# Hybrid mixer stage with its branches' work in another order, and one side step at every place of the dense stage

## The chip, the cores and the metric

The kernel is one program on one core of a Trainium2 chip. A core has a matrix engine (TensorE, PE in the profile), a vector engine (VectorE, DVE), an activation engine (ScalarE, ACT), a general engine (GpSimd, POOL), a queue engine that only issues transfers here (SyncE, SP), and 16 DMA engines that all of them share. The metric is the device time of one execution in microseconds, the median of several runs; less is better. Each engine runs its own instruction list in order, and they wait for each other through semaphores.

## The reference, cut to what matters

A sequence of 256 tokens of width 1024 passes through a hybrid mixer (gated linear attention beside a sparse attention of three branches), a dense feed-forward layer, a state-space mixer, a mixture of eight experts, and then two layers of another kind. The first four steps share a pattern:

```
def adaln(c, w, b):                      # shift, scale, gate from the condition vector c
    mod = jax.nn.silu(c) @ w + b
    return jnp.split(mod[:, None, :], 3, axis=-1)

for each of hybrid, dense, ssm, moe:
    shift, scale, gate = adaln(c, mod_w, mod_b)          # mod_w is 1024 x 3072
    x = x + gate * layer(rmsnorm(x, w) * (1 + scale) + shift)

gla:  log_alpha = log_sigmoid(lowrank @ gk_up + gk_bias) / 16;  b = cumsum(log_alpha) per chunk of 64
      q_dec = q * exp(b);  k_dec = k * exp(-b);  k_to_end = k * exp(b_end - b)
      o = intra-chunk + state part;  o = rmsnorm(o, out_norm) * silu(r)
nsa:  gate0 * compressed branch + gate1 * branch over selected keys + gate2 * window branch
      (compressed keys and values = gelu(blocks @ w1) @ w2)
mix:  concat([gla, nsa]) @ w_out
dense: (silu(g) * u) @ w_down,  g, u = split(h @ w_gu)   # 1024 -> 2 x 2816 -> 1024
```

## The kernel before, in words

All matrix products are done in two parts to keep float32 accuracy: a weight tile is split into a rounded high part by ScalarE (`split_hi`, uh in the profile) and the remainder by VectorE (`split_lo`, ul), and TensorE makes three products for each tile (high by high, high by low, low by high). The weights arrive in three slots of 2 MB, issued by SyncE; the pieces that are split are called units, and three units are in flight, so ScalarE can split unit n only when TensorE has used unit n - 3.

**The side job.** The shift, scale and gate of a layer need a product of one vector with a 1024 x 3072 matrix. It isn't done on TensorE but woven in beside the stage ahead of it. A generator for each of three engines walks through the jobs hyb, dense, ssm, moe (`side_gpsimd`, `side_vector`, `side_tensor`, lines 955 to 1048). A job has three parts (shift, scale, gate) of 8 chunks: GpSimd's queue loads a chunk of 512 KB into one of three buffers once VectorE is done with the chunk three back, VectorE adds it to `macc` with one instruction of 128x1024, and after the eighth chunk TensorE sums `macc` over the partitions (16 products of one column for shift or scale, `("cols", 0)` and `("cols", 1)`; two wide products for the gate, `"rows"`), and VectorE adds the bias. The bias of the gate is loaded into the buffer that held the last chunk, so only after VectorE has used that chunk.

**Its clock.** The generators go on by one `yield` at each call of `c.side_t.step()` and `c.side_v.step()` (class `Stepper`, line 417). `pace = (4, 5)` lets four of five calls through. `until(...)` goes on until the named result is there. TensorE and VectorE call it at the same logical places: in the hybrid stage at every tile and between the pieces of the attention, in the dense stage twice for each of the 22 gate and up units and once for each of the 22 row tiles of the down product. The state-space stage (`mamba`) begins on both engines with `until(("moe", "rows"))`, because its own buffers lie over those of the side job.

**The hybrid stage** (`hybrid`, line 1056). A loop over 24 input units calls `tile_*`, `gla_*` and `beside_*` on each engine; the numbers `Z, GATES, SCALED, STATE...` say at which unit a piece of the gated linear attention is issued. After that come `attention_tensor`, `attention_scalar`, `attention_vector`: three hand-written orders of calls for what is left of the two full branches (`br` 0 and 1), for the compressed branch and for its block product (`hidden_tensor`, 16 matmuls that use the weights `hyb_w1`). Then the output projection runs in quarters (`project_quarters`), for which the mixed result is turned (`mix_tensor`, `mix_scalar`, `mix_vector`), the first four columns of tiles ahead of it in `out_begin`, the other four after its third unit. GpSimd multiplies the heads of the linear attention by their norm (`Ogn`), then by the gate `r` (`gla`), and adds the two branch results (`nb`); between these it also issues the side job's loads, up to the points where `c.follow` lets it.

PSUM has eight banks. The turns of branch 1 and its scores take banks 0, 1 and 2 in turn (`bkb[1]`), the turns of the mixed result banks 0 and 1 (`bt`).

**The dense stage** (`dense`, line 1995): 22 gate and up units of 256 columns with 2 tiles of 24 matmuls each, then 11 down units of 2 row tiles with 12 matmuls of 512 columns each (`project_tensor`), then `gated_vector`, which adds the gated result to X in four quarters and begins the next stage's norm.

Of the kernel before, what the change touches and what calls it, by code (L numbers as in the profile page):

```python
# [1054 lines left out]
def hybrid(c):  # L1055
# [96 lines left out]
    def gpsimd(e):  # L1152
# [11 lines left out]
        og8 = Og[:, :, :, :].rearrange("p h a v -> p (h a) v")  # L1164
# [3 lines left out]
        c.follow(e, "hyb_in")  # L1168
        e.wait_ge(*v.at(("Og", 1, 1)))
        e.wait_ge(*a.at("gla_rst"))  # L1170
        e.tensor_tensor(og8, og8, bc(vs[:, :], 2, 128), ALU.mult).then_inc(*g.up("Ogn"))
        e.wait_ge(*g.at("Ogn"))
        e.tensor_tensor(mix[:, :, 0:512], Og[:, :, :, :].rearrange("p h a v -> p h (a v)"), rs[:, :, :], ALU.mult).then_inc(*g.up("gla"))
        c.follow(e, "hyb_attention")
        for hf in range(2):
            e.wait_ge(*v.at(("nb0", hf)))
            e.wait_ge(*v.at(("branch", 0, hf)))
            e.tensor_tensor(nb[0][:, hf, :], nb[0][:, hf, :], nb[1][:, hf, :], ALU.add).then_inc(*g.up(("nb", hf)))
# [96 lines left out]
    Z, GATES, SCALED, STATE, INSIDE, OUTER, NORM = 6, 7, 10, 14, 17, 19, 23  # L1275

    def gla_tensor(e, n):
# [8 lines left out]
        elif n == SCALED:  # L1286
# [49 lines left out]
    def gla_scalar(e, n):  # L1336
        if n == Z:
            e.table()
        elif n == GATES:
# [5 lines left out]
            e.activation(za[:, :, :], za[:, :, :], AF.Ln, bias=1.0).then_inc(*a.up("softplus"))  # L1345
            e.wait_ge(*v.at("be"))
# [3 lines left out]
            for f in range(2):  # L1350
# [3 lines left out]
    def norm_heads_scalar(e):  # L1354
# [7 lines left out]
        e.activation(vs[:, :], vs[:, :], AF.Exp, scale=-0.5).then_inc(*a.up("gla_rst"))  # L1362

    def gla_vector(e, n):
# [17 lines left out]
        elif n == SCALED:  # L1382
# [7 lines left out]
            e.tensor_tensor(k2[:, :, :], k2[:, :, :], za[:, :, :], ALU.mult).then_inc(*v.up("k2d"))  # L1390
            ps = c.psum.of("gla_ke")
# [229 lines left out]
    def compressed_out_vector(e):  # L1621
        e.wait_ge(*a.at("gla_rst"))
        for hf in range(2):
# [4 lines left out]
            c.psum.leave(("nsa_oc", hf), v)  # L1628

# [88 lines left out]
    def beside_tensor(e, m):  # L1718
# [11 lines left out]
        elif m == KV1 + 1:  # L1730
            branch_tensor(e, 0, 0)
            scores_tensor(e, 0, 1, 1)
            hidden_tensor(e, 1)
# [26 lines left out]
    def attention_tensor(e):  # L1760
        values_tensor(e, 1)
        turn_tensor_heads(e, 0, 1, 0)
        turn_tensor_heads(e, 0, 1, 2)
        c.side_t.step()
        scores_tensor(e, 1, 0, 0)
        scores_tensor(e, 1, 0, 1)
        turn_hidden_tensor(e)
# [3 lines left out]
        turn_tensor_heads(e, 1, 0, 0)  # L1771
        branch_tensor(e, 0, 1)
        c.side_t.step()
        turn_tensor_heads(e, 1, 0, 4)
        scores_tensor(e, 1, 1, 0)
        keys_tensor(e)
        c.side_t.step()
        branch_tensor(e, 1, 0)
        compressed_tensor(e)
        scores_tensor(e, 1, 1, 1)  # L1780
# [134 lines left out]
    def vector(e):  # L1915
# [21 lines left out]
        for hf in range(2):  # L1937
            factored = mix[:, hf, 512:1024]
            if hf:
                branch_vector(e, 1, 1)  # L1940
# [2119 lines left out]
```

## Time and profile before

| | us |
|---|---|
| median of 3 runs (2542.83 to 2543.85) | 2543.76 |
| the profiled execution, its own time | 2538.75 |
| its span in the profile | 2537.0 |
| TensorE busy in it | 2381.5 (94%) |
| VectorE busy | 1978.0 (78%) |
| ScalarE busy | 1458.9 (58%) |
| GpSimd busy | 226.0 (9%) |

The busy row of the page, in 40 slices of 63.4 us, shows where TensorE isn't full: `PE   5888899699989999999999999998999999899998`. The hybrid stage lies in slices 1 to 5, the dense stage in slices 5 to 8, and the low digit 6 stands in slice 8, where the dense stage ends and the state-space stage begins. The row of the granted clock is `PEclk 8897999799989999999999999999999999999999`.

The page's groups are over the whole program, and a change in the first 500 us hardly moves them. So the reading goes by stretches of time. In a timeline row the number in brackets is how long the engine was idle just before, and which instruction ended that.

### The profile page before, as it was taken

To read this page: it belongs to the slowest core of one execution; us is meant where nothing else is said; L and a number is where in the kernel's file an instruction comes from. 1 tells how busy PE (TensorE), PEld (TensorE's weight loads), DVE (VectorE), ACT (ScalarE), POOL (GpSimd) and SP (SyncE) were. 2 spreads that over 40 slices of the span, in tenths; PEclk is the share of its full clock that TensorE was granted. 3 is DMA by queue.
4 is the path that set the end of the run, shared out by engine and by line. 5 is a ranking of instruction groups with operands and counts; after the bars stand their busy time and mean duration, and the time that the engine had idled before them with its cause. 6 is when DMAs were issued, how large, how long until landed. Compare 5 with 4: busy or idle time off the path is not lost.

```text
span 2537.0 us, 33016 instructions
## 1 busy us (share of the span) xinstructions
PE 2381.5 (94%) x13939; PEld 2083.1 (82%) x13939; DVE 1978.0 (78%) x2132; ACT 1458.9 (58%) x1671; POOL 226.0 (9%) x275
## 2 busy tenths in 40 slices
PE   5888899699989999999999999998999999899998
PEld 4767898598878888888888888887888998887997
DVE  6656776689768999999999999986667875767875
ACT  3323533267647777767676777775456554455662
POOL 1101010101100000000000000000311211220110
PEclk8897999799989999999999999999999999999999
DMA  9562768634559999999999999995224554223551
GB/s 320 180 239 93 251 238 297 216 134 161 185 187 330 345 369 349 368 348 359 355 360 347 370 345 367 342 365 176 99 92 158 184 198 146 94 93 117 198 212 73
DMA packets 264886, 612.70 MB, mean 242 GB/s; under 512 B 18696, under 2 KB 33370, under 8 KB 264730
## 3 DMA queue, kind: packets, MB, share of 16 engines
q1 hardware_dynamic: 247824, 554.39, 60.7%
q0 software_dynamic: 15824, 55.72, 6.5%
q8 instruction: 111, 1.82, 0.3%
q10 hardware_dynamic: 1082, 0.40, 0.1%
q14 instruction: 45, 0.37, 0.0%
HBM read 609.40 MB, written 1.08 MB: 241 GB/s over the span
## 4 chain that ended last, share of the span: by engine, by line
PE 79%; DVE 11%; ACT 4%; DMA 3%; issue 2%; POOL 1%; SPq 0%; DVEq 0%; ACTq 0%; POOLq 0%
PE ps L132 77%; PE ps L136 2%; DVE eb L145 1%; DVE macc L153 1%; DVE gate L153 1%; DMA slots<-in_hyb_mod_w 1%; DVE ul_ssm_w L145 1%; DVE ul_moe_w L145 1%; ACT xn L139 1%; DMA beside<-in_dense_mod_w 1%; DVE xn L150 1%; DMA beside<-in_moe_mod_w 1%; ACT uh_moe_w L139 1%; DVE ul_in L145 0%; DVE xn L153 0%
## 5 line engine op out<-in xcount | busy, mean ns | idle before, releaser
L145 DVE TENSOR_TENSOR ul_moe_w<-slots,uh_moe_w 128x2048 fp32r<-128x2048 f32 x334 | 761.4, 2289 | 92.2 <-ACT uh_moe_w L139 91.8
L139 ACT ACTIVATE uh_moe_w<-slots 128x2048 fp32r<-128x2048 f32 x334 | 640.3, 1918 | 199.7 <-PE ps L132 170.4
L132 PE MATMUL ps<-uh_moe_w,XGh 128*128 128x512 f32 x896 | 354.7, 396 | 3.4 <-DVE XGl L145 2.1
L132 PE MATMUL ps<-uh_moe_w,XGl 128*128 128x512 f32 x896 | 349.5, 390 | 0.0
L132 PE MATMUL ps<-ul_moe_w,XGh 128*128 128x512 f32 x896 | 349.1, 390 | 0.0
L145 DVE TENSOR_TENSOR ul_ffn<-slots,uh_ffn 128x2048 fp32r<-128x2048 f32 x64 | 145.8, 2290 | 79.4 <-ACT uh_ffn L139 79.4
L132 PEld LDWEIGHTS ps<-uh_moe_w,XGh 128*128 128x128 f32 x896 | 168.3, 188 | 40.6 <-DVE ul_moe_w L145 5.2
L132 PE MATMUL ps<-HTf,uh_ffn 128*128 128x256 f32 x704 | 199.4, 283 | 2.0 <-DVE HTlf L145 2.0
L132 PE MATMUL ps<-HTlf,uh_ffn 128*128 128x256 f32 x704 | 199.2, 283 | 0.0
L132 PE MATMUL ps<-HTf,ul_ffn 128*128 128x256 f32 x704 | 199.2, 283 | 0.0
L132 PEld LDWEIGHTS ps<-uh_moe_w,XGl 128*128 128x128 f32 x896 | 168.2, 188 | 36.0
L132 PEld LDWEIGHTS ps<-ul_moe_w,XGh 128*128 128x128 f32 x896 | 168.4, 188 | 33.3
L132 PE MATMUL ps<-uh_moe_w,ehTh 128*128 128x512 f32 x448 | 177.3, 396 | 0.1
L132 PE MATMUL ps<-ul_moe_w,ehTh 128*128 128x512 f32 x448 | 174.6, 390 | 0.0
L139 ACT ACTIVATE uh_ffn<-slots 128x2048 fp32r<-128x2048 f32 x66 | 125.5, 1911 | 72.3 <-PE ps L132 72.1
L132 PE MATMUL ps<-uh_moe_w,ehTl 128*128 128x512 f32 x448 | 138.1, 389 | 0.0
L132 PEld LDWEIGHTS ps<-HTf,uh_ffn 128*128 128x128 f32 x704 | 135.1, 192 | 2.4 <-DVE HTlf L145 2.4
L132 PEld LDWEIGHTS ps<-HTf,ul_ffn 128*128 128x128 f32 x704 | 135.2, 192 | 0.0
L132 PEld LDWEIGHTS ps<-HTlf,uh_ffn 128*128 128x128 f32 x704 | 135.2, 192 | 0.0
L145 DVE TENSOR_TENSOR ul_dense_w<-slots,uh_dense_w 128x2048 fp32r<-128x2048 f32 x33 | 75.5, 2291 | 44.1 <-ACT uh_dense_w L139 44.1
L139 ACT ACTIVATE uh_dense_w<-slots 128x2048 fp32r<-128x2048 f32 x33 | 62.9, 1913 | 77.1 <-PE ps L132 76.9
L132 PE MATMUL ps<-HTm,uh_in 128*128 128x256 f32 (+1 forms) x336 | 101.8, 303 | 4.2 <-DVE ul_in L145 3.0
(530 smaller groups left out, 5551.8 us busy)
## 6 DMA issues: line engine op xcount, KB each, us to landing
slots<-in_moe_w_gu SPq DMA_DIRECT2D x111, 2048.0 KB, 9.1
slots<-in_moe_w_down SPq DMA_DIRECT2D x56, 2048.0 KB, 8.2
slots<-in_w_up SPq DMA_DIRECT2D x20, 2048.0 KB, 8.0
slots<-in_w_in SPq DMA_DIRECT2D x14, 2048.0 KB, 8.4
slots<-in_dense_w_gu SPq DMA_DIRECT2D x10, 2048.0 KB, 10.3
slots<-in_ssm_w_in SPq DMA_DIRECT2D x10, 2048.0 KB, 8.1
slots<-in_w_down SPq DMA_DIRECT2D x10, 2048.0 KB, 8.1
slots<-in_dense_w_down SPq DMA_DIRECT2D x5, 2048.0 KB, 11.6
```

The source lines that it names most:

```text
L132: return self.e.matmul(o, lhsT, rhs, start=start, stop=stop, skip_group_check=skip) if self.e else DONE
L136: return self.e.transpose(o, i, ident[0:n, 0:n]) if self.e else DONE
L139: return self.e.activation(o, i, f, **kw) if self.e else DONE
L145: return self.e.tensor_tensor(o, a, b, op) if self.e else DONE
L150: return self.e.tensor_scalar(o, a, s1, None, op0) if op1 is None else self.e.tensor_scalar(o, a, s1, s2, op0, op1)
L153: return self.e.scalar_tensor_tensor(o, a, s, b, op0, op1) if self.e else DONE
```

## The change

Nothing that is computed changes. What changes is on which engine, and in which order.

In the **dense** stage the pace of the side steps goes from four of five calls to every call, on TensorE and on VectorE.

In the **gated linear attention** ScalarE's exponentials, one block at unit 7 (`GATES`), are dealt out to units 7, 8, 9 and 10, and the turn of `Ee` on TensorE with its copy on VectorE moves from unit 10 (`SCALED`) to unit 12 (`TURNED`).

**Off GpSimd** go the norm of the heads (to ScalarE, 8 activations with a scale per partition, `scale_heads_scalar`), the product with the gate (to VectorE, one instruction of 128x1024, `gated_heads_vector`) and the two additions of the branches (to VectorE, 128x512 each). The two points at which GpSimd's side loads were held, `hyb_in` and `hyb_attention`, go too.

In the **attention** the scores of branch 1 and the turn of the values go into the last unit of the loop, ahead of the second block product; that product follows the first turns of branch 0; the turn of the first four tiles of the mixed result goes from behind the attention to the middle of its second half, ahead of the last turns of branch 1; and the last product of branch 1 goes ahead of the compressed branch's output. The six side steps of the attention stay six, at other places.

```
@@ def gpsimd(e) @@
-        c.follow(e, "hyb_in")
-        e.wait_ge(*v.at(("Og", 1, 1)))
-        e.wait_ge(*a.at("gla_rst"))
-        e.tensor_tensor(og8, og8, bc(vs[:, :], 2, 128), ALU.mult).then_inc(*g.up("Ogn"))
-        e.wait_ge(*g.at("Ogn"))
-        e.tensor_tensor(mix[:, :, 0:512], ... rs[:, :, :], ALU.mult).then_inc(*g.up("gla"))
-        c.follow(e, "hyb_attention")
-        for hf in range(2):
...
-            e.tensor_tensor(nb[0][:, hf, :], nb[0][:, hf, :], nb[1][:, hf, :], ALU.add)...
@@ gla @@
-    Z, GATES, SCALED, STATE, INSIDE, OUTER, NORM = 6, 7, 10, 14, 17, 19, 23
+    Z, GATES, SCALED, TURNED, STATE, INSIDE, OUTER, NORM = 6, 7, 10, 12, 14, 17, 19, 23
@@ def gla_tensor, gla_vector @@
-        elif n == SCALED:
+        elif n == TURNED:
             ps = bk2.take("gla_ke")
@@ def gla_scalar @@
             e.activation(za[:, :, :], za[:, :, :], AF.Ln, bias=1.0).then_inc(*a.up("softplus"))
+        elif n == GATES + 1:
             e.wait_ge(*v.at("be"))
...
-            for f in range(2):
+        elif GATES + 2 <= n < GATES + 4:
+            for f in (n - GATES - 2,):
                 for i in range(4):
                     e.activation(Ee[:, f, ...], cum[:, f, ...], AF.Exp, ...)
@@ new @@
+    def scale_heads_scalar(e):
+        og8 = Og[:, :, :, :].rearrange("p h a v -> p (h a) v")
+        e.wait_ge(*a.at("gla_rst"))
+        for i in range(8):
+            e.activation(og8[:, i, :], og8[:, i, :], AF.Copy, scale=vs[:, i:i + 1])...
+    def gated_heads_vector(e):
+        e.wait_ge(*a.at("Ogn"))
+        e.wait_ge(*g.at("rsn"))
+        e.tensor_tensor(mix[:, :, 0:512], ... rs[:, :, :], ALU.mult).then_inc(*v.up("gla"))
@@ def beside_tensor @@
             scores_tensor(e, 0, 1, 1)
-            hidden_tensor(e, 1)
+            values_tensor(e, 1)
+            scores_tensor(e, 1, 0, 0)
+            scores_tensor(e, 1, 0, 1)
@@ def attention_tensor, as it is after the change @@
         turn_tensor_heads(e, 0, 1, 0)
         turn_tensor_heads(e, 0, 1, 2)
         hidden_tensor(e, 1)
         c.side_t.step()
         turn_tensor_heads(e, 0, 1, 4)
         turn_tensor_heads(e, 0, 1, 6)
         turn_tensor_heads(e, 1, 0, 0)
         turn_tensor_heads(e, 1, 0, 4)
         turn_hidden_tensor(e)
         c.side_t.step()
         scores_tensor(e, 1, 1, 0)
         branch_tensor(e, 0, 1)
         c.side_t.step()
         branch_tensor(e, 1, 0)
         scores_tensor(e, 1, 1, 1)
         keys_tensor(e)
         c.side_t.step()
         compressed_tensor(e)
         c.side_t.step()
         mix_tensor(e, range(0, 4))
         turn_tensor_heads(e, 1, 1, 0)
         turn_tensor_heads(e, 1, 1, 2)
         c.side_t.step()
         turn_tensor_heads(e, 1, 1, 4)
         turn_tensor_heads(e, 1, 1, 6)
         turn_compressed_tensor(e)
         branch_tensor(e, 1, 1)
         compressed_out_tensor(e)
@@ def attention_vector, from the third side step on, as it is after the change @@
         scores_vector(e, 1, 1, 0)
         c.side_v.step()
         gelu_end_vector(e)
         branch_vector(e, 0, 1)
         branch_vector(e, 1, 0)
         scores_vector(e, 1, 1, 1)
         keys_vector(e)
         gated_heads_vector(e)
         c.side_v.step()
         compressed_vector(e)
         c.side_v.step()
         O.split_lo(e, 0)
         mix_vector(e, range(0, 4))
         factor_vector(e, 1, 1)
         c.side_v.step()
@@ dense, def tensor and def vector @@
-        c.side_t.pace = (4, 5)
+        c.side_t.pace = (1, 1)
-        c.side_v.pace = (4, 5)
+        c.side_v.pace = (1, 1)
```

## Rows read from the trace of the kernel before

**Rows 1.** Stretches: us, busy (x instructions) by engine, TensorE clock, DMA share, GB/s.

```profile
280.00:380.00 100.00, 99.28 (x830) 99.08 (x829) 73.44 (x72) 43.39 (x51) 11.08 (x21) 1.00 0.77 268
...
460.00:470.00 10.00, 10.00 (x46) 8.29 (x45) 4.27 (x4) 2.38 (x3) 2.08 (x4) 1.00 1.03 397
...
480.00:490.00 10.00, 0.00 (x0) 0.00 (x0) 6.32 (x5) 0.54 (x3) 2.64 (x5) 0.50 0.71 221
```

**Rows 2.** Timeline of TensorE, dense stage's end: start, us, what [idle before].

```profile
469.84 0.61 PE L132 MATMUL ps<-uh_dense_w,hTl 128*128 128x512 f32 x2
471.02 2.23 PE L132 MATMUL ps<-ones,macc 128*128 128x1 f32 x16 [0.56 <-DVE macc L153]
493.86 3.78 PE L132 MATMUL ps<-macc,ones 128*128 128x512 f32 x4 [20.61 <-DVE macc L153]
...
510.35 0.42 PE L132 MATMUL ps<-HT,uh_ssm_w 128*32 128x256 f32 x1
```

**Rows 3.** Timeline of VectorE, dense stage and its end.

```profile
378.19 2.28 DVE L145 TENSOR_TENSOR ul_dense_w<-slots,uh_dense_w 128x2048 fp32r<-128x2048 f32 x1
380.39 1.28 DVE L153 SCALAR_TENSOR_TENSOR macc<-beside,sc,macc 128x1024 f32<-128x1024 f32 x1
...
461.50 1.28 DVE L153 SCALAR_TENSOR_TENSOR macc<-beside,sc,macc 128x1024 f32<-128x1024 f32 x1 [1.82 <-DMA beside<-in_moe_mod_w]
...
469.59 1.29 DVE L153 SCALAR_TENSOR_TENSOR macc<-beside,sc,macc 128x1024 f32<-128x1024 f32 x1 [1.72 <-DMA beside<-in_moe_mod_w]
...
472.26 0.68 DVE L145 TENSOR_TENSOR xn<-ps,gate 128x512 f32<-128x512 f32 x1
...
478.17 0.69 DVE L145 TENSOR_TENSOR X<-X,xn 128x512 f32<-128x512 f32 x1
...
498.21 1.28 DVE L145 TENSOR_TENSOR gate<-gate,ps 128x512 f32<-128x512 f32 x2 [4.41 <-DMA gate<-in_moe_mod_b]
```

**Rows 4.** Timeline of GpSimd: the load of the last bias.

```profile
494.10 0.53 POOL L177 DMA_DIRECT2D gate<-in_moe_mod_b  x1 [5.54 <-DVE macc L153]
```

**Rows 5.** Timeline of TensorE: side products, and the way from hybrid to dense.

```profile
254.70 1.02 PE L132 MATMUL ps<-macc,ones 128*128 128x512 f32 x2
...
262.05 0.39 PE L132 MATMUL ps<-ul_hyb_in,xnr 128*128 128x512 f32 x1
...
273.44 0.39 PE L132 MATMUL ps<-HT,uh_dense_w 128*128 128x256 f32 x1 [1.36 <-DVE HTl L145]
...
435.53 1.92 PE L132 MATMUL ps<-ones,macc 128*128 128x1 f32 x16 [0.27 <-DVE macc L153]
```

**Rows 6.** Timeline of VectorE: the last addition to X in the hybrid stage.

```profile
266.37 0.69 DVE L145 TENSOR_TENSOR X<-X,xn 128x512 f32<-128x512 f32 x1
```

**Rows 7.** Timeline around the exponentials: VectorE, GpSimd and TensorE, each in its order.

```profile
68.62 3.12 DVE L153 SCALAR_TENSOR_TENSOR zb<-zb,za 128x512 f32<-128x512 f32 x1 [0.75 <-ACT za L139]
...
77.42 1.23 DVE L145 TENSOR_TENSOR ul_hyb_in<-slots,uh_hyb_in 128x1024 fp32r<-128x1024 f32 x1 [4.17 <-ACT uh_hyb_in L139]
...
68.79 2.39 POOL L145 TENSOR_TENSOR rs<-rs,onr 128x1024 f32<-128x1024 f32 x1
...
78.82 0.41 PE L136 MATMUL ps<-k_ident,gate 88*128 88x88 f32 x1 [6.27 <-DVE v_g L156]
87.23 1.09 PE L136 MATMUL ps<-k_ident,Ee 128*128 128x128 f32 x4 [3.16 <-DVE Ee L145]
```

**Rows 8.** Timeline of TensorE, second half of the attention.

```profile
217.56 0.69 PE L136 MATMUL ps<-k_ident,cs 128*128 128x128 f32 x2 [2.62 <-ACT cs L139]
...
225.72 0.77 PE L136 MATMUL ps<-k_ident,mix 128*128 128x128 f32 x4 [1.81 <-DVE xnr L145]
227.42 7.09 PE L132 MATMUL ps<-vb,PT 128*128 128x64 f32 x32 [0.93 <-DVE xnr L145]
234.26 0.77 PE L132 MATMUL ps<-ul_hyb_in,mixTh 128*128 128x512 f32 x1
```

**Rows 9.** A stretch of the attention, columns as in rows 1.

```profile
200.00:210.00 10.00, 10.00 (x65) 9.10 (x64) 4.94 (x16) 2.08 (x8) 1.26 (x3) 0.50 0.36 107
```

More of the change, by code:

```diff
@@ L1167, in gpsimd @@
         e.tensor_tensor(rs8, rs8, bc(onr[:, :], 1, 8), ALU.mult).then_inc(*g.up("rsn"))
[L1168 to L1178, printed above, removed]
         c.follow(e, "hyb_out")
@@ L1349, in gla_scalar @@
             e.activation(za[:, :, :], cum[:, :, :], AF.Exp, scale=-1.0 / 16).then_inc(*a.up("Ek"))
-            for f in range(2):
+        elif GATES + 2 <= n < GATES + 4:
+            for f in (n - GATES - 2,):
                 for i in range(4):
@@ L1362, in norm_heads_scalar, with scale_heads_scalar, gated_heads_vector @@
         e.activation(vs[:, :], vs[:, :], AF.Exp, scale=-0.5).then_inc(*a.up("gla_rst"))
+    def scale_heads_scalar(e):
+        og8 = Og[:, :, :, :].rearrange("p h a v -> p (h a) v")
+        e.wait_ge(*a.at("gla_rst"))
+        for i in range(8):
+            e.activation(og8[:, i, :], og8[:, i, :], AF.Copy, scale=vs[:, i:i + 1]).then_inc(*a.up("Ogn"))
+    def gated_heads_vector(e):
+        e.wait_ge(*a.at("Ogn"))
+        e.wait_ge(*g.at("rsn"))
+        e.tensor_tensor(mix[:, :, 0:512], Og[:, :, :, :].rearrange("p h a v -> p h (a v)"), rs[:, :, :], ALU.mult).then_inc(*v.up("gla"))
     def gla_vector(e, n):
@@ L1628, in compressed_out_vector @@
             c.psum.leave(("nsa_oc", hf), v)
+        for hf in range(2):
+            e.wait_ge(*v.at(("nb0", hf)))
+            e.tensor_tensor(nb[0][:, hf, :], nb[0][:, hf, :], nb[1][:, hf, :], ALU.add).then_inc(*v.up(("nb", hf)))
     def scores_tensor(e, br, hf, gi):
@@ L1792, in attention_scalar @@
         weights_scalar(e, 0, 1, 1)
-        hidden_scalar(e, 1)
         turn_scalar_heads(e, 0, 1, 0)
@@ L1866, in mix_vector @@
             c.psum.leave(("hyb_mT", k), v)
-    def out_begin(e):
-        mix_tensor(e, range(4))
-        branch_tensor(e, 1, 1)
     def out_after(e, n):
@@ L1885, in tensor @@
         attention_tensor(e)
-        project_quarters(c, e, S, O, mh, ml, 0, [[k] for k in range(8)], lambda k: v.at(("ml", k)), [[5, 6], [7, 2]], out_begin, out_after)
+        project_quarters(c, e, S, O, mh, ml, 0, [[k] for k in range(8)], lambda k: v.at(("ml", k)), [[5, 6], [7, 2]], None, out_after)
         c.side_banks = c.banks
@@ L1906, in scalar @@
         O.split_hi(e, 2)
-        mix_scalar(e, range(4))
         O.split_hi(e, 3)
@@ L2021, in tensor @@
         turn_tensor(c, e, S, xn, [v.at(("xn", 0)), v.at(("xn", 1))], (6, 5))
-        c.side_t.pace = (4, 5)
+        c.side_t.pace = (1, 1)
         for n in range(NU):
@@ L2084, in vector @@
             U.split_lo(e, n)
-        c.side_v.pace = (4, 5)
+        c.side_v.pace = (1, 1)
         for n in range(AHEAD, len(U) + AHEAD):
```

80 lines of the change are left out of this document (40 added, 40 removed).

## The prediction, made before the changed kernel was run

> **What bounds the kernel now.** I began with the page: TensorE is busy 94% of the span, so nearly everything later than 520 us is its own work, which the change doesn't touch. What can move lies in the slices with lower digits, the hybrid stage and the end of the dense stage. Next I read the stretches [rows 1]: in 280 to 380 us TensorE is full, at the full clock, and VectorE has 27% to spare; in 480 to 490 us TensorE makes not one product. Then the timelines of both engines there. The last dense product ends at 469.84 + 0.61 = 470.45; after a short sum at 471.02 TensorE is idle for 20.61 us and waits for `macc` [rows 2]. The first state-space product stands at 510.35, 39.9 us behind the last dense one. From hybrid to dense the same passage takes from 262.05 + 0.39 = 262.44 to 273.44, 11.0 us [rows 5]. So some 29 us of this passage belong to no data that the next stage's input needs: it is the side job for moe, drained with `until`, at the speed at which its chunks come in. The reader is to see two more places: TensorE idle for 6.27 and 3.16 us around the exponentials [rows 7], and for 2.62, 1.81 and 0.93 us in the second half of the attention [rows 8], which moreover runs at 0.50 of the clock, its lower level of 1.2 GHz [rows 9].
>
> **Part 1, the side steps in the dense stage.** This is counting, from the generators. A job of three parts has 2 + (1 + 8) + ... places: the parts with columns take 10 steps each, the gate part 11, the start 2, so 33. The hybrid stage calls 24 times at tiles, 9 in the linear attention, 6 in the attention and 8 behind it, 47 in all, which is 14 for hyb (one part, its first step included) and 33 for dense; it ends even. The dense stage calls 2 x 22 + 22 = 66 times. At four of five that is 53 steps; ssm takes 33 of them and moe 20. 13 steps are left for `until`: the end of moe's scale part, its whole gate part of 8 chunks, and its sum. The trace agrees: VectorE takes scale's last chunk at 469.59 and does the gate part behind the additions to X, up to the bias at 498.21 [rows 3]. At every call there are 66 steps for 66: the last moe chunk falls on the down tile 18, the result on tile 21, the last. Nothing is left to drain.
>
> What it costs. TensorE makes the same sums, but now inside its stream: one sum over columns (1.92 us [rows 5]; it stood at 471.02 in the passage) and the gate's two wide products (one took 1.02 us at the full clock [rows 5], so 2.0). Its dense end moves from 470.45 to 474.4. VectorE then has: last chunk, about 465 (tile 18 lies some 5 us ahead of the end in its order; it waits for the transfer, see below); the bias, which can be issued only then and took from 494.10 to 498.21, 4.1 us [rows 3, 4], so 469 to 473 with other traffic; the two gate additions, 1.28 us [rows 3]; the two small weight splits, which filled the time from 470.88 to 472.26, 1.4 us [rows 3]. So it starts on X at 474 to 476, about when the last product is there. Before, it started at 472.26 and was through at 478.17 + 0.69 = 478.86, 6.6 us [rows 3]; from the last addition to X to the next stage's first product took 267.06 to 273.44 in the other passage, 6.4 us [rows 5, 6]. That gives 487 to 489 for the first state-space product against 510.35, 21.4 to 23.4 us. That first tile ran partly at half the clock behind the long idle time (0.42 us a product [rows 2]); without it, about 1 us more. Stalls inside the dense stage take off 0 to 3. **I take 22.5 us, with 16 and 26 as the bounds.**
>
> The cover. Between 280 and 380 us a product takes 100 / 830 = 0.12 us [rows 1], so a pair of units, 96 products, 11.5 us. VectorE then has two splits (2.20 us from start to start), four chunks (1.28 each) and four of 128x256, about 0.34 each by half of the 0.68 of a 128x512 [rows 3]: 10.9 us, 95%. It is close, but a unit's split is wanted only two units later, so a delay of some us is taken up. In the down part a tile has 12 products of 512 columns, 2.7 us, at 46 products in 10 us [rows 1]; a unit of two tiles asks 2.2 + 2 x 1.28 = 4.8 of 5.4 us of VectorE. If the cover were gone, each us that a chunk comes late would be an us of TensorE.
>
> The transfers decide that. In the down part weights ask for 2 MB in four tiles (10.9 us, 193 GB/s) and chunks for 0.52 MB a tile, another 193. 386 GB/s together. At 460 to 470 us the trace shows 397 GB/s, with chunks starting at 461.50 and 469.59, three apart, 2.70 us each, and waits of up to 1.82 us before them [rows 1, 3]. So the pace wanted is just what the queue gave at its fullest: little or no room, but 16 such tiles only, with two gaps of two and more, and a lead of some 6 us. From this come the 0 to 3 us.
>
> The Trainium skill, page "DMA: Bandwidth & Descriptors", section "Bandwidth", puts HBM to SBUF at about 358 GB/s for a core. By it a tile with its chunk would take 2.9 instead of 2.7 us, and the 16 tiles 3 to 4 us more, about the lead; the trace's 397 GB/s over 10 us speaks against the figure for a single busy core, and I go by the trace.
>
> **Part 2, the exponentials.** ScalarE waited at unit 7 for `be`, made eleven exponentials, and only then split unit 8; VectorE was idle for 4.17 us for that split, and TensorE for 6.27 us for a small copy behind it [rows 7]. After the change ScalarE splits unit 8 before it waits. VectorE is ready when `cum` and `be` are, at 77.42 - 4.17 = 73.25, and goes straight on: all of 4.17 us comes off. The idle time left, some 2 us, is short; the tile behind it ran at half the clock, and I give 1 to 2 us for that. The wait of 3.16 us for `Ee` goes, as TensorE comes to the turn two units later, with VectorE long done; the turn itself stays (1.09 us). What is late next is VectorE, with about 2.9 us for each tile of 2.9. That makes 4.2 + 3.2 + 1 less about 1.4 for VectorE's closeness: **7 us, bounds 3 and 9** (the low end if the wait for `Ee` only moves).
>
> **Part 3, the attention.** The work of TensorE is the same, so the gain is idle time less new idle time. Removed: at most 2.62 + 1.81 + 0.93 = 5.4 us [rows 8]. New: `mix_tensor` for tiles 2 and 3 needs banks that VectorE leaves only after the compressed scores, a chunk (1.28), an output split (1.23, as at 77.42 [rows 7]) and a 128x256 subtraction (0.34), so TensorE, with everything of branch 1's last half queued behind it, stands for about 3 us. Also new: VectorE's third side step now lies ahead of the gelu's end, and waits until TensorE has done branch 0's product. In its favour: VectorE loses the long waits beside GpSimd. Where GpSimd multiplied at 68.79, VectorE's 128x512 instruction took 3.12 us [rows 7], where one of the same size at 472.26 took 0.68 [rows 3], and the two GpSimd multiplications of the attention go. (The Trainium skill, page "SBUF — State Buffer", calls the port pair of these two engines an exclusive lock, where the loser blocks for the whole instruction; by that rule, the trace agrees, all of that loss comes back where the GpSimd work goes, and stays at 68.62, where it doesn't.) In exchange VectorE gets one instruction of 1.3 and two of 0.7, ScalarE eight short ones of 128x128; both have idle time there, 4.94 and 2.08 us busy of 10 [rows 9]. The wide products of the compressed output now stand right before the projection, which began at half the clock (0.77 us [rows 8]), so 1 to 2 us may come from that. 5.4 - 3.4 + 2: **4 us, bounds -2 and 10**, the upper one if the half clock of [rows 9] sets in later. The GpSimd queue, no longer held, issues side loads earlier; no wait for them stood here, so nothing.
>
> **Sum.** 22.5 + 7 + 4 = 33.5 us. The profiled execution took 2538.75, so 2505.3; the median of the runs stands 5.0 us above it, and I keep that: 2510.
>
> **The rivals.**
> *B, side transfers too slow in the dense stage.* Chunks come at 3 us or more, VectorE waits in front of splits, TensorE stands. For it: 386 GB/s asked, waits at 461.50 (and by the Trainium skill's 358 GB/s, above, it would be the likeliest of all, at its lower end). Against: the average over 280 to 380 is 268 GB/s, a fifth more chunks makes 300. Costs 5 to 12 of the 22.5: 2515 to 2522, say 2518. Chance 0.17.
> *C, the attention's new waits win.* The turn of the mixed tiles and the side step cost more than they save, 0 to 6 us lost instead of 4 gained: 2514 to 2520, say 2517. Chance 0.14.
> *D, the clock.* The attention and the tiles around the exponentials stay at the full clock; 20 us of it at half cost about 10: 2498 to 2503, say 2501. Chance 0.11.
> *E, slower than before.* VectorE, at 95% in the gate and up units, becomes the bound because each chunk waits for its transfer in front of the splits. A pair of units has 0.6 us to spare; with a wait w at each of its four chunks TensorE loses 4w - 0.6 in each of 11 pairs. That eats the whole 33.5 us at w = 0.9 us; at w = 1.3 the loss is 51 us, 17 more than the gain: 2561. For it: waits of 1.8 us do occur [rows 3]; against: only where chunks run back to back. Chance 0.02.
> *F, the steps don't end in the dense stage,* because a wait holds VectorE's generator back, so that part of the drain stays, half of the 22.5: 2521. Chance 0.04.
>
> **How the numbers follow.** The forecast has what is left, 0.52: 2510, itself 2504 to 2516. The range takes in D's lower part (the upper bounds of the three parts together would give 2499) and goes to the upper part of B and F: 2499 to 2523; it leaves out some 2 in 10, odd mixtures of B, C and F above all. 0.2% (5 us, about what a measurement of this kernel can tell from no change) is passed by all but E and a bad mixture of B and C: faster 0.96, same 0.02, slower 0.02.
>
> **What would show it.** Right: no idle time of TensorE over 3 us between the last dense and the first state-space product, and these 12 to 15 us apart; moe's last chunk before the last dense product; 280 to 380 us with VectorE above 85% and TensorE still at 99%; first V product 7 us earlier; projection of the hybrid stage 9 to 13 us earlier. Wrong: TensorE waiting for `ul_dense_w` (B, E); a wait of over 5 us at the turns of `mix` (C); `until` still with chunks in it (F).

## The result and the profile after

The changed kernel takes 2508.44 us (median of 4 runs, 2507.7 to 2510.34) against 2543.3 of the kernel before beside it: a ratio of 0.987, 95% interval 0.9855 to 0.9886. On two more chips the same kernel stood at 0.9886 (0.9869 to 0.9903) and 0.9896 (0.9882 to 0.9911). The three ratios are worth 33, 29 and 26 us. One execution of the kernel before (7537.53 us) and one of the kernel called step first below (2974.25 us) stand far outside the others and are left out of the ratios. The forecast was 2510, range 2499 to 2523. The time came out where it was forecast. Two of its three terms did not, and most of their errors cancelled.

The profiled execution took 2508.9 us (before: 2538.75). From its page, the span, the busy times and three rows of the span in 40 slices:

```profile
span 2507.1 us, 33025 instructions
...
PE 2365.5 (94%) x13939; PEld 2069.0 (83%) x13939; DVE 1976.4 (79%) x2135; ACT 1460.5 (58%) x1679; POOL 218.5 (9%) x271
...
PE   5898999899989999999999999998999999899998
...
PEclk8998999999989999999999999999999999999999
DMA  9754777544559999999999999995124554223551
```

The hole in TensorE's row at the end of the dense stage is gone. The timeline of TensorE there, which answers to [rows 2] (start, us, what, idle time before and its releaser in brackets):

```profile
467.95 0.61 PE L132 MATMUL ps<-uh_dense_w,hTl 128*128 128x512 f32 x2
468.40 2.84 PE L132 MATMUL ps<-k_ident 128*128 128x128 f32 x24
472.30 1.09 PE L136 MATMUL ps<-k_ident,xn 128*128 128x128 f32 x8 [1.06 <-DVE xn L150]
473.23 1.28 PE L132 MATMUL ps<-k_ident 128*128 128x128 f32 x10
476.16 1.09 PE L136 MATMUL ps<-k_ident,xn 128*128 128x128 f32 x8 [1.65 <-DVE xn L150]
480.04 2.77 PE L132 MATMUL ps<-k_ident 128*32 128x128 f32 x12 [2.79 <-ACT xn L139]
482.74 0.31 PE L132 MATMUL ps<-HT,uh_ssm_w 128*32 128x256 f32 x1
```

From the last dense product's end (467.95 + 0.61) to the first state-space product are 14.2 us. Before they were 39.9 (510.35 less 469.84 + 0.61 [rows 2]). In the two other executions of this kernel that were traced they were 15.8 and 15.7. The 20.61 us wait for `macc` no longer stands there. But the dense stage itself, from its first product to its last, took 212.0 us (256.58 to 468.56) where it had taken 197.0 (273.44 [rows 5] to 470.45 [rows 2]). TensorE's waits in it, by what it waited for (us in total, times, longest):

```profile
PE ps L132 <- DVE macc L153: 7.1, 4, 2.2
```

Two stretches of the stage, columns as in [rows 1]:

```profile
262.00:362.00 100.00, 98.85 (x804) 97.71 (x803) 76.18 (x77) 41.16 (x48) 13.16 (x25) 0.98 0.82 290
390.00:400.00 10.00, 7.95 (x38) 7.16 (x37) 7.30 (x10) 2.79 (x4) 0.58 (x2) 0.70 1.00 400
```

Over most of the stage TensorE is busy. In the second stretch it is busy 7.95 of 10 us, its clock at 0.70 and the DMA engines full. That stretch holds a column sum, which TensorE reached 2.05 us before VectorE had finished the chunk that it sums:

```profile
393.77 3.30 PE L132 MATMUL ps<-ones,macc 128*128 128x1 f32 x16 [2.05 <-DVE macc L153]
```

The other three waits stand at 320.25 (1.15 us waited), 427.98 (1.70) and 458.08 (2.21). The granted clock of the stage, read in steps of 4 us, adds up to about 14 us at its lower level, 0.50, where the kernel before had 3.4. A stretch at half clock costs half of its length, so the 15.0 us by which the stage grew can be added up, as an estimate: 6.1 us more of waits for `macc` (7.1 less 1.0 before), some 5 us of half clock, and the 3.9 us of sums that the prediction had moved into the stage, 15 in all. So the side steps' own gain is 25.7 us at the passage less 15.0 in the stage, 10.7. The first dense product came 16.9 us earlier, and the first state-space product, taking both, 27.6.

### The profile page after: what moved, and what is told of

It reads as the page before. It is cut to its first block, busy times and chain, and to the rows that moved or that the text cites. A ratio compares the mean times of both kernels' runs of the same rounds, so it can differ in the third digit from the quotient of the medians.

```text
span 2507.1 us, 33025 instructions
## 1 busy us (share of the span) xinstructions
PE 2365.5 (94%) x13939; PEld 2069.0 (83%) x13939; DVE 1976.4 (79%) x2135; ACT 1460.5 (58%) x1679; POOL 218.5 (9%) x271
## 4 chain that ended last, share of the span: by engine, by line
PE 72%; DVE 14%; DMA 6%; ACT 5%; issue 2%; POOL 1%; SPq 0%; DVEq 0%; ACTq 0%; POOLq 0%
PE ps L132 70%; PE ps L136 2%; DMA slots<-in_moe_w_gu 2%; DVE ul_moe_w L145 2%; DVE macc L153 1%; DVE eb L145 1%; ACT uh_moe_w L139 1%; DVE gate L153 1%; DMA beside<-in_moe_mod_w 1%; DVE ul_ssm_w L145 1%; DMA slots<-in_hyb_mod_w 1%; ACT xn L139 1%; DMA beside<-in_dense_mod_w 1%; DVE xn L150 1%; DVE xn L153 0%
## 5 line engine op out<-in xcount | busy, mean ns | idle before, releaser
L145 DVE TENSOR_TENSOR ul_dense_w<-slots,uh_dense_w 128x2048 fp32r<-128x2048 f32 x33 | 75.5, 2289 | 34.9 <-ACT uh_dense_w L139 34.9
```

What stands on the lines that cost most here:

```text
L145: return self.e.tensor_tensor(o, a, b, op) if self.e else DONE
```

## The experiments

The table below orders the runs by what their traces show: start of the hybrid projection, of the first dense and the first state-space product (us from the span's start), and the distance of the last two. Where a run was repeated, the rows are separate executions of the same kernel.

| kernel | projection | dense | state space | distance | ratio to before |
|---|---|---|---|---|---|
| before | 234.3 | 273.4 | 510.4 | 237.0 | 1 |
| exponentials only | 224.6 | 264.6 | 500.6 | 236.0 | 0.9964 |
| hybrid parts only | 215.2 | 254.6 | 491.4 | 236.8 | 0.9926 |
| side steps only | 233.4 | 272.7 | 504.0 | 231.3 | 0.9965 |
| after | 216.9 | 256.6 | 482.7 | 226.1 | 0.987 |
| after, again | 222.7 | 262.4 | 488.7 | 226.3 | 0.9886 |
| after, third | 214.9 | 254.4 | 483.1 | 228.7 | 0.9896 |
| step first | 215.6 | 255.0 | 474.0 | 219.0 | 0.9862 |
| step first, again | 215.5 | 254.8 | 471.2 | 216.4 | 0.987 |
| half chunks | 215.1 | 256.0 | 472.3 | 216.3 | not comparable |
| mix late | 221.6 | 261.5 | 493.2 | 231.7 | 0.9908 |
| norm on GpSimd | 217.0 | 257.2 | 482.7 | 225.5 | 0.9883 |
| fill the wait | 213.0 | 253.9 | 468.6 | 214.7 | 0.9852 |

**Hybrid parts only.** The changed kernel with the paces of the dense stage as before:

```
-        c.side_t.pace = (1, 1)        (and side_v)
+        c.side_t.pace = (4, 5)
```

> The changed kernel with the dense stage's side steps back at 4 places in 5 (both paces), so that only the two hybrid parts are left. Reading of the two traces: the first dense product came 16.9 us earlier, the side steps gave 10.7 us net, so this kernel should stand 15 to 19 us below the kernel before (2524 to 2528), its passage from dense to ssm near 40 us again. The prediction's own sum (hybrid parts 7 + 4 = 11 us, side steps 22.5): 2532. If the parts depend on each other (a hybrid stage that ends earlier moves the chunks' transfers onto others), neither.

2520.59 us against 2540.58 on its chip, ratio 0.9926 (0.9912 to 0.994): 19 us less, 15 to 22. The prediction's sum, 11 us, lies outside. The distance between the first dense and the first state-space product is the old one, 236.8, so all of it is gained before the dense stage. The parts were forecast too small, while the other expectation on record, 15 to 19 us from the traces, was about right.

**Side steps only.** The kernel before with the two paces at (1, 1), the same two lines the other way round.

> The kernel before with only the dense stage's side steps at every place. Reading of the traces: 10.7 us less than before (2531 to 2534): the passage loses some 25 us, the dense stage grows by some 15 us, TensorE waiting for macc at the sums. The prediction's sum: 22.5 us less, 2521, the dense stage growing by 4 to 7 us.

2529.69 us, ratio 0.9965 (0.9953 to 0.9978): 9 us less, 6 to 12. The 22.5 of the prediction lies outside. The passage is down to 16.1 us, as forecast, and the stage up from 197.0 to 215.2. TensorE waits for `macc` as in the changed kernel:

```profile
PE ps L132 <- DVE macc L153: 7.1, 5, 1.9
```

The two halves add up: 0.9926 and 0.9965 make 28 us, the whole change 26 to 33. So the side steps lose this much with the hybrid stage as it was, too: the loss doesn't come from the hybrid stage's earlier end.

**Exponentials only.** The kernel before with the gates' decay exponentials in three units and the turns two units later:

```
+        elif n == GATES + 1:
             e.wait_ge(*v.at("be"))
...
+        elif GATES + 2 <= n < GATES + 4:
+            for f in (n - GATES - 2,):
...
-        elif n == SCALED:    (gla_tensor; in gla_vector the copy of gla_ke)
+        elif n == TURNED:
```

> The kernel before with only the gate exponentials over three units and the turns two units later. Prediction: 7 us less (2536). Reading of the traces: 12 us less at the first attention product of branch 0, of which 7 are work waited for and the rest a clock that stays full over 70 to 100 us; if all of that is kept, 2531. If the attention stage eats the gain (its waits are set by something other than where it begins), under 3 us.

2529.58 us, ratio 0.9964 (0.995 to 0.9978): 9 us less, 6 to 13, for a forecast of 7. The trace shows how it came. The kernel's first stop behind the exponentials shrank from 6.27 us (at 78.82 [rows 7]) to the 2.02 us that the changed kernel shows too:

```profile
75.01 0.29 PE L136 MATMUL ps<-k_ident,gate 88*128 88x88 f32 x1 [2.02 <-DVE v_g L156]
```

Branch 0's first product then came at 160.27, 12.9 us before the 173.16 of the kernel before, and the projection 9.7 us before. What is lost between lies in the attention, which from branch 0's first product to the projection took 64.4 us for 61.1 before. Its waits there are the same, and its clock isn't: here it was 0.50 from 180 us on, where the kernel before still had 1.00 up to 196.

**VectorE's step first.** In the changed kernel VectorE's first side step of each dense unit goes ahead of the unit's low split:

```
         for n in range(AHEAD, len(U) + AHEAD):
+            m = n - AHEAD
+            c.side_v.step()
             if EARLY <= n < len(U):
                 U.split_lo(e, n)
-            m = n - AHEAD
...
                 for f in range(2):
-                    c.side_v.step()
+                    if f:
+                        c.side_v.step()
```

> The changed kernel with VectorE's first side step of each dense unit ahead of its low split instead of behind it. In the trace VectorE waited 34.9 us in 20 waits for ScalarE's high half ahead of that split, with a chunk landed or not behind it. If VectorE's order makes the chunk late at the sums: the four waits of TensorE for macc (7.1 us) shrink to under 2 us and the time falls by 5 to 10 us (2498 to 2503). If the transfers make it late: the same waits, and the time within 2 us of 2508; if the splits then come late, slower, with TensorE waiting for ul_dense_w.

2503.64 us on its chip, ratio 0.9862 (0.9846 to 0.9878). As this is close to the changed kernel's first ratio, both were run once more side by side:

> The changed kernel once more, so that the two kernels beside it are compared on one chip: 2505 to 2512. In its trace TensorE's clock should return to 1.00 either near 210 us, and the hybrid projection begin near 217, or near 222, and the projection begin near 222, as in the two executions of it so far.

> VectorE's side step ahead of the low split, on the same chip as the changed kernel. If its first result was the edit's doing: 5 to 9 us under the changed kernel beside it, the dense stage near 203 us instead of 210 to 212. If it was that execution's clock: within 2 us of it.

The changed kernel gave 2514.09 (2509.78 to 2515.58), above the 2505 to 2512 expected, and its projection began at 214.9, earlier than either of the two places expected. The step first gave 2505.3 (four runs of it 2502.86 to 2510.36), 8.8 us less, with ratios of 0.9896 (0.9882 to 0.9911) and 0.987 (0.9852 to 0.9887). These two intervals still touch. The traces are clearer than the times: the distance is 216.4 and 219.0 us with the step first, and 226.1, 226.3 and 228.7 without. The dense stage itself took 202.7 and 200.0 us with it, against 212.0, 210.5 and 212.9. The waits of TensorE in the dense stage with the step first (its first run):

```profile
PE ps L132 <- DVE macc L153: 1.5, 2, 1.1
```

These waits are about half of the gain, and the clock is most of the rest. Side by side, on one chip, the waits were 8.1 us in the changed kernel and 2.0 with the step first, and the stretches at half clock some 14 us and none. That is 6 and 7 us, for the 12.9 by which the stages differ.

Why the waits shrank, is seen in VectorE's timeline ahead of the sum at 393.77 of the changed kernel:

```profile
389.15 2.29 DVE L145 TENSOR_TENSOR ul_dense_w<-slots,uh_dense_w 128x2048 fp32r<-128x2048 f32 x1
392.33 1.28 DVE L153 SCALAR_TENSOR_TENSOR macc<-beside,sc,macc 128x1024 f32<-128x1024 f32 x1 [0.90 <-DMA beside<-in_moe_mod_w]
```

and ahead of the same sum with the step first, which TensorE began at 388.30:

```profile
386.87 1.29 DVE L153 SCALAR_TENSOR_TENSOR macc<-beside,sc,macc 128x1024 f32<-128x1024 f32 x1 [3.51 <-DMA beside<-in_moe_mod_w]
388.07 2.28 DVE L145 TENSOR_TENSOR ul_dense_w<-slots,uh_dense_w 128x2048 fp32r<-128x2048 f32 x1
```

In both the chunk's transfer is late. In the changed kernel the split (2.29 us) and the wait (0.90) stand one behind the other ahead of the chunk, and TensorE's sum needs that chunk. With the step first VectorE waits longer for the transfer, 3.51 us, but in the main in time that it had spent waiting for ScalarE's high half anyway: those waits fall from 34.9 to 24.5 us. VectorE's waits in the two traces, the changed kernel and then the step first:

```profile
DVE ul_dense_w L145 <- ACT uh_dense_w L139: 34.9, 20, 6.3
DVE macc L153 <- DMA beside<-in_moe_mod_w: 8.4, 5, 2.9
...
DVE macc L153 <- DMA beside<-in_ssm_mod_w: 5.2, 3, 2.2
```

```profile
DVE ul_dense_w L145 <- ACT uh_dense_w L139: 24.5, 16, 4.7
DVE macc L153 <- DMA beside<-in_moe_mod_w: 9.6, 3, 3.5
...
DVE macc L153 <- DMA beside<-in_ssm_mod_w: 3.9, 2, 2.0
DVE macc L153 <- DMA gate<-in_moe_mod_w: 3.0, 1, 3.0
```

**Half chunks.** Which leaves the other suspect, the transfers. The changed kernel, with the chunks of ssm and moe cut in two:

```
+                wd = 512 if name in ("ssm", "moe") else D
-                e.dma_start(bufs[n % 3], w[k * 128:(k + 1) * 128, part * D:(part + 1) * D])
+                e.dma_start(bufs[n % 3][:, 0:wd], w[k * 128:(k + 1) * 128, part * D:part * D + wd])
```

> The changed kernel with the chunks of the ssm and moe modulation loaded only for 512 of their 1024 columns (the other half of each buffer keeps what was there: this leaves half of that weight out of the result; all arithmetic stays). If the transfers make VectorE late at the sums: VectorE's waits for the ssm and moe chunks (13.6 us) fall under 4 us, TensorE's waits for macc (7.1 us) under 3 us, the bias wait of 6.3 us ahead of the first gated sum shrinks, and the time falls by 8 to 14 us. If VectorE's own order and load do: those waits of TensorE stay at 5 us or more and the time falls by under 4 us.

Its whole time, 3524.75 us, says nothing: this kernel leaves half of that weight out of the result, and the expert stage behind it executed more work (18531 TensorE instructions where the changed kernel has 13939). Up to the state-space stage the instructions are the same, and there the trace is to be read. TensorE waited for `macc` once:

```profile
PE ps L132 <- DVE macc L153: 1.1, 1, 1.1
```

VectorE's waits for these chunks' transfers fell from 13.6 to 6.4 us, not under 4 as expected; the bias wait of 6.3 us only to 5.7; the distance from 226.1 to 216.3, and the stage to 201.1 us. The chunks that go through `beside` had come to take longer from issue to landing with the change. The DMA issues of ssm's between 270 and 455 us, of before, of the changed kernel and of half chunks (count, KB each, median us to landing):

```profile
beside<-in_ssm_mod_w POOLq DMA_DIRECT2D x14, 512.0 KB, 5.8
```

```profile
beside<-in_ssm_mod_w POOLq DMA_DIRECT2D x12, 512.0 KB, 7.5
```

```profile
beside<-in_ssm_mod_w POOLq DMA_DIRECT2D x12, 256.0 KB, 6.3
```

This doesn't hold for every chunk: those of ssm's that go through `gate` took 4.9 us before and 5.0 after. So late transfers are a cause, and VectorE's order is what turned them into a stop of TensorE: taking away either one gives about the same 10 us.

**The changed kernel again, the mix late, the norm on GpSimd.** Three kernels on one chip.

> The changed kernel once more, unaltered, so that the three kernels beside it have it on the same chip: 0.987 of the kernel before (2505 to 2510), in the trace four waits of TensorE for macc in the dense stage (7 us).

It took 2510.12 us (ratio 0.9886), with three waits for `macc` (5.3 us) where four (7) were expected, and its profiled execution reached the projection at 222.7 where the first had it at 216.9, by the same instructions in the same order. TensorE's timeline in the first execution and in this one:

```profile
205.66 1.12 PE L136 MATMUL ps<-k_ident,mix 128*128 128x128 f32 x4 [3.68 <-DVE xnr L145]
...
211.95 3.76 PE L132 MATMUL ps<-vb,PT 128*128 128x64 f32 x32 [1.32 <-ACT PT L139]
215.54 1.94 PE L132 MATMUL ps<-vbd,ct 128*128 128x512 f32 x4
```

```profile
206.83 1.12 PE L136 MATMUL ps<-k_ident,mix 128*128 128x128 f32 x4 [3.66 <-DVE xnr L145]
...
213.11 7.06 PE L132 MATMUL ps<-vb,PT 128*128 128x64 f32 x32 [0.56 <-ACT PT L139]
219.97 3.73 PE L132 MATMUL ps<-vbd,ct 128*128 128x512 f32 x4
```

At the turns of the mix the two are 1.2 us apart. Then branch 1's product takes 3.76 us in one and 7.06 in the other, and the compressed output 1.94 and 3.73, about twice each: the granted clock over 210 to 220 us was 1.00 in the first and 0.50 in the second. So the projection began 5.8 us later, 4.6 of them from there on, in two executions of one kernel.

The mix late puts the first four mix turns, with their halves, behind the last head turns of branch 1 on the three engines:

```
-        mix_tensor(e, range(0, 4))
         turn_tensor_heads(e, 1, 1, 0)
...
         turn_tensor_heads(e, 1, 1, 6)
+        mix_tensor(e, range(0, 4))
         turn_compressed_tensor(e)
```

> The changed kernel with the turns of the first four mix pieces, with their high and low halves, behind the last head turns of branch 1 on all three engines. TensorE waited 3.7 us at them for the gated heads. If that wait is lost time: 2 to 5 us less. If what comes next waits for the same VectorE (the weights of branch 1, the compressed rows), the wait moves and the time stays within 1.5 us; if the low halves of the mix come late for the projection, 1 to 3 us more.

2516.29 us, ratio 0.9908 (0.9893 to 0.9923) against 0.9886 for the changed kernel beside it: no gain, 6 us more by the medians, and none of the three expectations gave that. The 3.68 us wait went and waits of 0.23, 1.29 and 1.44 us came in its place. In its trace the clock is at 0.50 from 190 until after 222 us as in the execution just shown, though TensorE is idle 1.3 us less on the way from branch 0's first product (5.8 against 7.1), and the projection begins at 221.6, 1.1 us earlier than there. So none of the 6 us lies in the attention. They are in the dense stage, which took 217.3 us against 210.5: TensorE waited 7.7 us for `macc` instead of 5.3, and some 24 us of the stage were at half clock instead of 10, which by half of the difference is 7 us. Why an edit ahead of that stage shifted its waits and its clock isn't shown; two executions of the changed kernel alone differ by 2.4 us there.

The norm on GpSimd moves the scaling of the heads and the gate product back:

```
-            e.activation(og8[:, i, :], og8[:, i, :], AF.Copy, scale=vs[:, i:i + 1]).then_inc(*a.up("Ogn"))
...
+        c.follow(e, "hyb_in")
+        e.tensor_tensor(og8, og8, bc(vs[:, :], 2, 128), ALU.mult).then_inc(*g.up("Ogn"))
```

> The changed kernel with the gated-linear heads' norm and gate back on GpSimd (the two additions of branch outputs stay on VectorE). If the shared port and GpSimd's slower operations were what the change removed: 3 to 6 us more, with the mix turns waiting for GpSimd instead of VectorE and VectorE's operations beside it longer. If ScalarE's and VectorE's new work costs what it saves: within 1.5 us, or less.

2509.54 us, ratio 0.9883, against 0.9886: the same. The traces say less, as this one was at half clock for some 28 us between 186 and 218 and the one beside it for 34. GpSimd's two multiplications lie at 182.50 and 184.47 us, and VectorE's gap ahead of 186.26 is a wait for TensorE:

```profile
182.50 1.89 POOL L145 TENSOR_TENSOR Og<-Og,vs 128x1024 f32<-128x1024 f32 x1 [11.83 <-ACT vs L139]
184.47 2.35 POOL L145 TENSOR_TENSOR mix<-Og,rs 128x1024 f32<-128x1024 f32 x1
...
186.26 0.17 DVE L145 TENSOR_TENSOR s_dense<-ps,v_m 128x8 f32<-128x8 f32 x1 [3.44 <-PE ps L132]
```

In the new order they fall into time in which VectorE has next to nothing to do, and taking them off GpSimd brought nothing. In the kernel before they did meet VectorE:

```profile
195.87 1.89 POOL L145 TENSOR_TENSOR Og<-Og,vs 128x1024 f32<-128x1024 f32 x1 [21.55 <-ACT vs L139]
197.84 2.35 POOL L145 TENSOR_TENSOR mix<-Og,rs 128x1024 f32<-128x1024 f32 x1
...
197.93 2.29 DVE L145 TENSOR_TENSOR fac<-sm,gt 128x8 f32<-128x8 f32 x1
...
220.68 0.17 DVE L145 TENSOR_TENSOR fac<-sm,gt 128x8 f32<-128x8 f32 x1
```

The same small instruction took 2.29 us beside the second of them and 0.17 away from them. But TensorE didn't wait between 191 and 214 us there, so that loss stood in nobody's way either. The attention's gain then comes from its new order, with one part not tried alone: the two additions of the branches, which stayed on VectorE.

**Filling the wait.** On top of the step first, products of the identity with itself between the second and the third mix turn, written to a bank that nobody reads:

```
             m.then_inc(*t.up(("mT", k)))
+            if k == 1:
+                ps = bkb[0].take("fill")
+                e.wait_ge(*ps.was)
+                idle_products(c, e, ps.t[:, 0:128], 12)
+                e.matmul(ps.t[:, 0:128], K["ident"][:, :], K["ident"][:, :]).then_inc(*t.up("fill"))
```

> As e4, and with 13 products of the identity with itself (128x128, written to a bank that nobody reads) between the second and the third turn of the mix, where TensorE waits 3.7 us for VectorE at half clock. They need 3.6 us at that clock and so fill the wait. If the idle time holds the clock down: the clock is back by 212 us, the projection begins by 218 in every execution, and the time is 0 to 4 us under the kernel with the step first. If the clock doesn't answer to it: the projection begins at 217 or 222 as before and the time is the same or up to 1 us more. If the products delay the turns (at full clock they need 1.7 us, at half more than the wait): 1 to 2 us more.

2501.11 us, ratio 0.9852 (0.9835 to 0.987), the lowest median of all, against 2505.3 and 0.987 for the step first beside it. The intervals overlap, so the 4 us are not clear of the scatter. The trace of TensorE:

```profile
198.73 4.30 PE L132 MATMUL ps<-k_ident 128*128 128x128 f32 x26
202.86 0.60 PE L136 MATMUL ps<-k_ident,mix 128*128 128x128 f32 x4
204.18 2.00 PE L136 MATMUL ps<-k_ident,S 128*128 128x128 f32 x16 [0.71 <-DVE xnr L145]
```

The third and fourth turns take 0.60 us here, 1.12 in the changed kernel and in the step first. The granted clock over 200 to 210 us, last but two of these columns, was 0.93, and 0.60 in the step first beside it (0.50 to 0.62 in the nine traces of the new order without the products):

```profile
200.00:210.00 10.00, 7.67 (x61) 7.17 (x61) 7.87 (x16) 5.82 (x13) 1.05 (x2) 0.93 0.35 105
```

```profile
200.00:210.00 10.00, 4.83 (x25) 3.75 (x23) 8.89 (x23) 4.49 (x10) 1.05 (x2) 0.60 0.34 102
```

The projection began at 213.0, 2.5 us before that of the step first beside it. That looks like the gain of the products, but most of it was there ahead of them. Branch 0's first product, where the two kernels are still the same, stands at 158.79 here:

```profile
158.79 1.90 PE L132 MATMUL ps<-vb,PT 128*128 128x64 f32 x16
```

and in the step first 2.4 us later:

```profile
161.15 1.90 PE L132 MATMUL ps<-vb,PT 128*128 128x64 f32 x16
```

From the first mix turn to the projection it is 15.2 us against 16.0, 0.9 us less, and that is what can be put down to the products. Between the projection and the first dense product this was lost again (40.9 us against 39.3; the clock fell to 0.50 once more, near 225 us, and did not in the step first). So these traces don't show that the products pay. The 4 us of the medians arose elsewhere in the main, or are scatter.

## Why the prediction was right, and where it wasn't

**The whole.** 33.5 us were forecast, and by the three ratios 26 to 33 came. By its parts the sum would have been 28 to 30: side steps 9 to 11 (the run with them alone, and 10.7 from the traces), exponentials 9, attention 10 (hybrid parts only less exponentials only, 0.9926 to 0.9964). The side steps were forecast some 12 us too high and the other two some 8 too low together. That 2508.44 lies so close to 2510 is luck: the first chip's ratio was the best of the three, and the 5.0 us that were added for the median over the profiled execution are scatter (the changed kernel's two are 0.5 us apart, the other way). Of rival B, put at 0.17, the mechanism came in the main, and of rival D, put at 0.11, a good part.

**Part 1, the side steps: 22.5 forecast, about 10 measured, below its lower bound of 16.** The passage was right, or nearly: 14.2, 15.8 and 15.7 us in three executions for a forecast of 12 to 15, no wait of TensorE over 3 us in it, moe's last chunk at 456.74, before the last dense product. The extra sums were right too: with the late chunks nearly cured, the dense stage took 202.7 and 200.0 us (step first, twice), 5.7 and 3.0 more than before, for 3.9 forecast. The mis-sized term is that of the stalls: 0 to 3 us stood there, and 9.3 to 12.9 were spent (212.0 less 202.7, and 212.9 less 200.0 for the two that ran side by side). In the first trace 7.1 us are waits for `macc`; the half clock behind them, such as the 0.70 over 390 to 400 us, a term that the prediction didn't have in this stage, makes most of the rest.

The reason against rival B, an average of 300 GB/s, was the failing step. An average of 290 was measured indeed, but what counts is the stretch ahead of a sum: 400 GB/s and the DMA engines full over 390 to 400 us, and the two `beside` chunks issued between 385 and 395 us took 7.0 us to land, by their median. B's mechanism was at work beside the forecast's. But it works through the sums alone. TensorE never waited for `ul_dense_w`, so rival E's chain, a wait in front of each split, wasn't seen. Nor was VectorE as near its limit as the prediction had it: 76% of 262 to 362 us, under the 85% that it named as a sign and the 95% of its sum. The sum counted a chunk for each step, four in a pair of units, but a job has 24 chunks in its 33 steps, 2.9 for four steps. So it wasn't a lack of VectorE's time that made the chunks late.

The prediction had set the Trainium skill's 358 GB/s ("DMA: Bandwidth & Descriptors", § Bandwidth) against 397 measured [rows 1]. The changed kernel's trace again shows more than that figure, 400 GB/s over 10 us.

**Part 2, the exponentials: 7 forecast, 9 measured (6 to 13).** What was late next was VectorE, as said, and the 3.12 us instruction beside GpSimd stayed (3.13 us at 68.91). At branch 0's first product the gain was 12.9 us with the exponentials alone: 7.4 are the waits (6.27 less 2.02, and the 3.16 for `Ee`, which is gone), and about 5 the clock, at 1.00 over 70 to 100 us, where the kernel before had 0.83, 0.67 and 0.99. The prediction gave the clock 1 to 2. Some 3 us of the 12.9 were lost again in the attention.

**Part 3, the attention: 4 forecast, 10 measured, at the end of its range.** The 10 are what it adds to the exponentials. From branch 0's first product to the projection it took 61.1 us before, 64.4 with the exponentials alone, and 54.3 to 59.2 in the nine traces of the new order without the products in the wait. The projection was forecast 9 to 13 us earlier and came 17.3, 11.5 and 19.3 earlier in three executions of the changed kernel. The new wait at the mix turns was forecast at 3 us and was 3.68. The removal of 5.4 us of idle time didn't come: TensorE's waits between branch 0's first product and the projection are 7.9 us in all (7.1 before), 1.57 of them a new one for `vb` at 168.04. So by its idle time the new order gains nothing. The gain lies in the stretch at half clock, which lasted from about 196 to 237 us before, with some 3 us of full clock near 225, and from about 189 to 210 in the changed kernel's first trace (to 224 in its second, to 208 in its third). Rival D had named the clock, and only as an addition; it was the main part. The clause that VectorE loses its waits beside GpSimd was true and worth nothing here: in the kernel before there was such a wait, and TensorE didn't stand for it; in the new order the norm's multiplications fall where VectorE is idle, so the Trainium skill's exclusive lock ("SBUF — State Buffer", § SBUF: two separate sides) has nobody to block, and the run with them back on GpSimd is as fast. Where the two engines do meet, at 68.91, the trace agrees with the page.

Why the clock returned earlier in the new order stays open. One trace, with a wait filled, had it back at about 201 us instead of 207 to 224, which speaks for idle time as what holds it down. But the mix late had 1.3 us less idle time than the changed kernel beside it, and its clock came back no sooner. What makes the clock fall near 189 us, with TensorE busy 10.00 of 10 over 180 to 190, wasn't tried.

## What to carry to other kernels

Side work spread over a stage costs what its sums wait for, not what its chunks take: look at the instruction that joins it to the main engine, and put the chunk ahead of the work it would otherwise stand behind, so that its wait for a transfer falls into a wait that is there anyway. Judge a stage's room for more transfers by the fullest 10 us, not by its average. Moving work off an engine pays only where the other engine is held by it; look for its name beside a longer instruction first, and then for a wait of the main engine behind that. And when two traces differ behind an edit, look how far they were apart ahead of it.

## What the runs showed of the chip

The granted clock isn't a property of the program alone: with the same instructions in the same order, and 1.2 us apart, it returned to 1.00 near 210 us in one execution and after 222 in another, which cost 4.6 us. Differences of that size between two traces need the clock row before they need an explanation. Short waits seem to cost more than their length: in the dense stage 7.1 us of waits for `macc` came with some 14 us at half clock, and with the step first 1.5 us came with 7 in one execution, and 2.0 with none in another. Useless products of TensorE in a wait (4.30 us in all, 26 records for 13 products) went with a clock of 0.93 instead of 0.60 over the 10 us in which they lie, and with 0.9 us gained there, in one trace; that they pay isn't shown. And a chunk of 512 KB that GpSimd's queue loads into `beside` for ssm took 5.8 us to land before and 7.5 after, though the stage moved only 12% more bytes in the same stretch (252 and 281 GB/s), while the chunks for `gate` took 4.9 and 5.0.
